# Two attentions in one fused kernel: heads issued in pairs, values as the stationary operand, constant rows moved into the second MLP

## The chip, the cores and the metric

The kernel runs on one core of one Trainium2 chip. The metric is the device time of one execution in microseconds (us). The core has a matrix engine (TensorE, PE in the profile, with its weight loads on a row of their own, PEld), a vector engine (VectorE, DVE), a scalar engine (ScalarE, ACT), GpSimd (POOL) and SyncE (SP), which issues all DMAs here. Each has its own queue, in order, and they meet by semaphores. [...]

## The reference

Three models of one layer each follow one another on 1024 positions of 1024 channels, all in fp32: a gated linear attention block with an MLP, a block with two attentions, a convolution and a gated MLP, and a block of spatial gating and pooling with an MLP. The change is in the second. Its attentions are these:

```python
def forgetting_attention(q, k, v, log_f):          # "fox": 6 heads of 64, blocks of 128 queries
    c = cumsum(log_f)                              # per head, over positions
    s = q @ k.T / 8 + c[query] - c[key]; s = where(key <= query, s, -inf)
    return softmax(s) @ v

def dilated_branch(q, k, v, window, dilation):     # (128, 1), (512, 4), (2048, 16)
    # blocks of window // dilation positions taken at steps of dilation, each with the one before
    s = where(band & ~first, q @ k.T / 8, -inf)
    m = max(s); e = exp(s - m); l = sum(e)
    return e @ v, m, l

def dilated_mixture(q, k, v):                      # 6 heads of 64
    a_p = exp(m_p - max_p(m_p))                    # weight of each of the three branches
    return sum_p(a_p * num_p) / sum_p(a_p * l_p)
```

Both outputs (384 channels each) go through an RMS norm with gains, are joined with 256 channels of the convolution and multiplied by w_o. Then comes an MLP of 2 x 2816 channels up and 2816 down. The third model's projections have a bias made of sums over rows of weights times the vector `mod`; there are 44 blocks of such weights, the constant rows.

## The kernel before, in words

Activations stand with channels on partitions and 1024 positions along the free side. A large product is a `job`: for each of 8 blocks of 128 channels three products of split parts (whi by hi, whi by lo, wlo by hi; L449, L450, L455) into one of three PSUM slots of two banks, `ps[0..2]`, taken in turn by `take`. A further slot of two banks, `misc`, holds small things. Weights come through a ring of four buffers `raw`; ACT rounds them into `whi` and POOL makes `wlo`.

The dilated attention (L719 to L778 on PE) has 72 units, `DUN`: a branch, a block of queries, a pair of heads. Unit n has its scores (two heads in the halves of the rows, L728), the mask added by a matmul of an identity with `negm` (L731), the maximum on DVE (L1832), the exponential with its sum on ACT from PSUM (L1242), transposes on PE (L716), a copy to SBUF on ACT or DVE (L1228, L1446), and the product with the values (L746). In the last, the transposed weights are stationary (128 columns) and 64 channels of values stream, so the output has positions on partitions. PE issues the scores of unit n, the transposes of n - 2 and the values of n - 3 in one step. Every three units a block of 128 positions by 384 channels, with maxima and sums, goes to DRAM through the three tiles `T` (24 stores). Six gate groups (`cn`, L754) and 44 row sums lie between the units: POOL multiplies a block of weights by `mod` and folds it with three additions (L2160), and PE sums over partitions with a column of ones (L774).

Fox (L781 to L829) has 48 units, `FUN`: a block of queries i (from 7 down to 0) and one head, against i + 1 blocks of keys. It has scores (L791), the causal mask (L792), gates and maximum in one DVE instruction (L1866), exponential on ACT (L1267), i + 1 transposes, copies and values (L803). Beside it run the eight `join` steps that read the dilated blocks back from DRAM, mix the three branches (POOL, L2160), and turn them on PE (L810), as are fox's own outputs. Norm factors are spread over channels by `spread` (L476): DVE first makes a diagonal block product of 1024 columns (`diag`, L1468), and PE multiplies it by ones. This helper is used for the norms of all three models.

The order of every queue is written out by hand, by the same loops over the same lists on each engine; the only freedom is what a wait leaves. The first model's MLP takes 48 blocks `ada` along, of the same kind as the constant rows, at the places `ADA_AT`: POOL multiplies, DVE sums over k (L1701), PE sums over partitions with ones (L630).

## Time and profile before

| | us |
|---|---|
| median of 3 runs (lowest, highest) | 3929.88 (3917.98, 3930.02) |
| the profiled execution's own time | 3927.38 |
| its span | 3925.5 |
| PE busy | 3749.1 (96%) |
| DVE / ACT / POOL busy | 1551.9 (40%) / 1006.5 (26%) / 1373.6 (35%) |
| mean granted clock of PE | 0.933 |

The page cuts the span into 40 slices of 98 us and gives each one digit, in tenths. PE stands at 9 in nearly all. The line of the granted clock (`PEclk`) reads 9 in most, and 8, 6, 5, 9 and 5 in the five slices between 1570 and 2061 us; the attentions lie between 1614 and 2045 us. A busy PE at a clock of 0.5 does half of the work in a microsecond. The chain that ended last is 89% PE.

One fp32 matmul of the source is two instructions in the trace, each a weight load and a stream that takes two passes over its columns. Durations of PE instructions overlap; what one costs is the distance from start to start.

### The profile page before, as it was taken

The numbers are of one execution on the slowest core, as the hardware profiler recorded it, in microseconds if no ns is written. First come the engines' busy times: TensorE is split into PE (matmuls) and PEld (weight loads), VectorE is DVE, ScalarE is ACT, GpSimd is POOL, SyncE is SP. The second block draws the span as 40 slices with busy tenths as digits, with TensorE's granted clock in tenths as the row PEclk, the third lists the DMA queues.
The fourth block names the chain that finished last, engine by engine and source line by source line (L and its number), as shares of the span: only waits on it lengthen the run. The fifth ranks groups of instructions, "written<-read, shape, count | busy, mean of one in ns | idle before, by whom it ended". The sixth has DMA issues, their size and how long they took to land.

```text
span 3925.5 us, 39427 instructions
## 1 busy us (share of the span) xinstructions
PE 3749.1 (96%) x16958; PEld 3039.1 (77%) x16958; DVE 1551.9 (40%) x1446; ACT 1006.5 (26%) x1460; POOL 1373.6 (35%) x786
## 2 busy tenths in 40 slices
PE   7999899999999999999989999999999979999997
PEld 5787678888888777777768778888877758888885
DVE  4444334333333466222434443433345351222224
ACT  4221122111111311343432322222242332222211
POOL 2111124444444422487322323332244343333332
PEclk9898889999999999865959999999999979999998
DMA  2011222222222211244102111111111111111112
GB/s 93 27 54 38 81 75 68 89 83 90 81 85 83 86 62 43 90 128 135 38 15 77 41 51 49 39 51 57 38 63 38 43 65 49 47 46 47 49 49 108
DMA packets 86107, 250.29 MB, mean 64 GB/s; under 512 B 9367, under 2 KB 18343, under 8 KB 85677
## 3 DMA queue, kind: packets, MB, share of 16 engines
q1 hardware_dynamic: 85932, 247.77, 19.1%
q8 instruction: 134, 2.20, 0.2%
q14 instruction: 41, 0.33, 0.0%
HBM read 224.52 MB, written 23.22 MB: 63 GB/s over the span
## 4 chain that ended last, share of the span: by engine, by line
PE 89%; DVE 6%; ACT 2%; POOL 2%; issue 1%; DMA 0%; SPq 0%; DVEq 0%; ACTq 0%
PE ps L449 25%; PE ps L455 25%; PE ps L450 25%; PE ps L791 2%; PE ps L716 2%; PE ps L803 1%; PE ps L746 1%; PE ps L728 1%; PE ps L542 1%; POOL raw L2160 1%; DVE T L1440 1%; PE ps L476 1%; DVE HL L1456 1%; DVE T L1465 1%; PE ps L607 1%
## 5 line engine op out<-in xcount | busy, mean ns | idle before, releaser
L2154 POOL TENSOR_TENSOR wlo<-raw,whi 128x1024 fp32r<-128x1024 f32 (+3 forms) x368 | 697.3, 1895 | 1836.1 <-ACT whi L926 1675.5
L449 PE MATMUL ps<-HH,whi 128*128 128x512 f32 (+2 forms) x2816 | 1125.7, 400 | 69.5 <-DVE HL L1456 30.7
L450 PE MATMUL ps<-HL,whi 128*128 128x512 f32 (+2 forms) x2816 | 1113.2, 395 | 0.0
L455 PE MATMUL ps<-HH,wlo 128*128 128x512 f32 (+2 forms) x2816 | 891.6, 398 | 0.0
L926 ACT ACTIVATE whi<-raw 128x1024 fp32r<-128x1024 f32 (+3 forms) x368 | 311.5, 847 | 1896.5 <-PE ps L455 1866.3
L449 PEld LDWEIGHTS ps<-HH,whi 128*128 128x128 f32 (+2 forms) x2816 | 536.2, 190 | 202.1 <-DVE HL L1456 29.5
L449 PE MATMUL ps<-GH,whi 128*128 128x512 f32 x1600 | 628.6, 393 | 7.9 <-POOL wlo L2154 7.8
L450 PEld LDWEIGHTS ps<-HL,whi 128*128 128x128 f32 (+2 forms) x2816 | 536.0, 190 | 116.6 <-issue 3.0
L450 PE MATMUL ps<-GL,whi 128*128 128x512 f32 x1600 | 623.6, 390 | 0.0
L455 PEld LDWEIGHTS ps<-HH,wlo 128*128 128x128 f32 (+2 forms) x2816 | 525.0, 190 | 105.1
L455 PE MATMUL ps<-GH,wlo 128*128 128x512 f32 x1600 | 494.1, 390 | 0.0
L1440 DVE TENSOR_TENSOR X<-ps,X 128x1024 f32<-128x1024 f32 x184 | 224.9, 1223 | 563.6 <-PE ps L455 560.0
L449 PEld LDWEIGHTS ps<-GH,whi 128*128 128x128 f32 x1600 | 301.7, 189 | 72.4 <-issue 10.5
L455 PEld LDWEIGHTS ps<-GH,wlo 128*128 128x128 f32 x1600 | 301.1, 188 | 62.9
L450 PEld LDWEIGHTS ps<-GL,whi 128*128 128x128 f32 x1600 | 301.2, 188 | 62.3 <-issue 0.8
L2160 POOL TENSOR_TENSOR GL<-T,GH 128x1024 fp32r<-128x1024 f32 x86 | 206.8, 2406 | 354.8 <-ACT GH L1127 236.8
L1451 DVE TENSOR_TENSOR T<-ps,RT 128x1024 f32<-128x1024 f32 x72 | 88.0, 1223 | 353.5 <-PE ps L455 319.4
L1701 DVE TENSOR_REDUCE adat<-raw 128x128 f32<-128x1024 f32 x48 | 97.0, 2022 | 236.1 <-POOL raw L2160 236.1
L1443 DVE SCALAR_TENSOR_TENSOR T<-T,cols,T 128x1023 f32<-128x1023 f32 x88 | 136.8, 1554 | 59.5 <-ACT T L1323 58.0
L1440 DVE TENSOR_TENSOR T<-ps,RT 128x1024 f32<-128x1024 f32 (+2 forms) x34 | 41.6, 1224 | 289.3 <-PE ps L455 260.5
L1127 ACT ACTIVATE GH<-T 128x1024 fp32r<-128x1024 f32 x64 | 68.0, 1062 | 269.1 <-DVE T L1440 269.1
L1440 DVE TENSOR_TENSOR T<-T 128x1024 f32<-128x1024 f32 (+3 forms) x74 | 112.7, 1523 | 40.2 <-ACT T L1119 39.1
(323 smaller groups left out, 3428.9 us busy)
## 6 DMA issues: line engine op xcount, KB each, us to landing
raw<-in_w_up SPq DMA_DIRECT2D x76, 512.0 KB, 3.3
raw<-in_w_in SPq DMA_DIRECT2D x70, 512.0 KB, 3.3
raw<-in_w_fc SPq DMA_DIRECT2D x64, 512.0 KB, 3.4
raw<-in_w_down SPq DMA_DIRECT2D x104, 256.0 KB, 2.7
raw<-in_w_ada SPq DMA_DIRECT2D x48, 512.0 KB, 3.5
raw<-in_w_fc SPq DMA_DIRECT2D x64, 256.0 KB, 2.7
X<-in_xT SPq DMA_DIRECT2D x16, 512.0 KB, 7.2
raw<-in_w_out SPq DMA_DIRECT2D x16, 512.0 KB, 3.3
```

Source lines behind the costliest of these rows:

```text
L449: e.matmul(o_[0:m, half(hf)], whi_[:, k, :], hi[k0 + k][:, half(hf)], start=first, stop=False)
L450: e.matmul(o_[0:m, half(hf)], whi_[:, k, :], lo[k0 + k][:, half(hf)], start=False, stop=False)
L455: i = e.matmul(o_[0:m, half(hf)], wlo_[:, k, :], hi[k0 + k][:, half(hf)], start=False, stop=last)
L716: i = e.transpose(o_[:, blk(j)], src[:, blk(j)], ident[:])
L791: e.matmul(o_[:, 512 * hf:512 * hf + k], QA[r_, t_, blk(i_)], KA[r_, t_, 512 * hf:512 * hf + k], start=True, stop=hf != (P * i_) // 512)
L926: e.activation(whi_of(name), raw_of(name), ACT.Copy).then_inc(*ac.inc("hi " + name))
L1440: e.tensor_tensor(o, a, b, op).then_inc(*dv.inc(*names))
L1443: e.scalar_tensor_tensor(out=o, in0=a, scalar=s_, in1=b, op0=op0, op1=op1).then_inc(*dv.inc(*names))
L1451: e.tensor_tensor(dst, ps[slot[g]][:], RT[:], MUL).then_inc(*dv.inc("free " + g, *names))
L1701: e.tensor_reduce(adat[:, f % 2, :], raw_of(f"ada{f}").rearrange("p (k m) -> p m k", k=8), AX.X, ADD).then_inc(*dv.inc(f"red ada{f}"))
L2154: e.tensor_tensor(wlo_of(name), raw_of(name), whi_of(name).bitcast(F), SUB).then_inc(*po.inc("lo " + name))
L2160: e.tensor_tensor(o, a, b, op).then_inc(*po.inc(*names))
```

## The change

- Dilated units run with eight blocks of one branch and head pair after the other. The mask matmul goes: DVE reads scores from PSUM and the mask from SBUF in one instruction per head, which writes the negated masked scores to SBUF and their minimum to `ML`. ACT takes the exponential from SBUF, in place. Scores alternate between `ps[0]` and `ps[1]`, transposes use the halves of `ps[2]`.
- Values are stationary (64 columns), the transposed weights stream (128 columns), the two heads go to the two halves of the output partitions. Outputs have channels on partitions and are copied into `NUM` at their positions; only maxima and sums go through DRAM (`msc`), 36 numbers per position.
- Fox runs by pairs of heads and halves of the queries, `FUN`, in 36 steps over the key blocks, `FSTEP`. Scores of both heads alternate; the exponentials of four query blocks lie in SBUF (`PF`); a step turns one key block for up to four query blocks and both heads, ACT copies the one head and DVE the other, and values are stationary with up to 512 columns streaming. The first four score pairs go behind the last dilated units.
- Mixing weights, softmax sums and norm factors are spread over channels by matmuls that take a broadcast column as stationary and the identity as moving operand, one such group in most steps (`FSIDE`); DVE multiplies them in. `spread` takes the same form for all norms of the kernel, and `diag` goes everywhere.
- The constant rows go into the second MLP at `ROW_AT`, in the way of `ada`; their loads stand there in the order of the weights.

```diff
+ROW_AT = [n for n in range(3, 62) if n % 4]
...
-DUN = [(br, u, t_) for br in range(3) for u in range(8) for t_ in range(3)]
-FUN = [(i, hd) for i in range(7, -1, -1) for hd in range(6)]
+DUN = [(br, t_, u) for br in range(3) for t_ in range(3) for u in range(8)]
+DSEQ = []
+for _n in range(len(DUN)):
+    DSEQ.append(("unit", _n))
+    if _n % 12 == 5:
+        DSEQ.append(("gate", _n // 12))
+FUN = [(t_, qd) for t_ in range(3) for qd in (1, 0)]
+FSTEP = [(k, j) for k in range(6) for j in range(8 if FUN[k][1] else 4)]
+FSCORE = {}
+for _k in range(5):
+    for _x, _i in enumerate(range(4 * FUN[_k + 1][1] + 3, 4 * FUN[_k + 1][1] - 1, -1)):
+        FSCORE[FSTEP.index((_k, 2 * _x + 1 if FUN[_k][1] else _x))] = (_k + 1, _i)
+FSIDE = {}
+_spread = [("mix", t_, br, hf) for t_ in range(3) for br in range(3) for hf in range(2)]
+for _n, (_k, _j) in enumerate(FSTEP):
+    if _k and _j == 0:
+        FSIDE[_n] = [("out", _k - 1)]
+    elif _n > 1 and _spread:
+        FSIDE[_n] = [_spread.pop(0)]
+_late = [n for n in range(len(FSTEP)) if n > max(n for n in FSIDE if FSIDE[n][0][0] == "mix") + 2 and n not in FSIDE]
+FSIDE[_late[2]] = [("rd sum",)]
+FSIDE[_late[3]] = [("rd", 0)]
+FSIDE[_late[4]] = [("rd", 1)]
+FSIDE[33], FSIDE[34] = [("rf sum", 1)], [("rf", 1)]
+SIDES = [x for n in sorted(FSIDE) for x in FSIDE[n]] + [("out", 5), ("rf sum", 0), ("rf", 0)]
...
+        def by_act(n):
+            br, t_, u = DUN[n]
+            return has_prev(br, u) == 1 and u % 3 == 0
...
+        def before_scores(k, i_):
+            if (k, i_) == (0, 7):
+                return dv("dm71")
+            lo = 4 * FUN[k][1]
+            if i_ < lo + 3:
+                return dv(f"fm{k} {i_ + 1}")
+            return dv(f"fm{k - 1} {4 * FUN[k - 1][1]}")
...
+            def spread(g, r, tok):
+                o_ = take(g)
+                q.wait_ge(*tok)
+                for b in range(8):
+                    i = e.matmul(o_[:, blk(b)], r[:, b:b + 1].broadcast_to([P, P]), ident[:], start=True, stop=True)
                 i.then_inc(*pe.inc(g))
...
             def dscores(n):
-                br, u, t_ = DUN[n]
+                br, t_, u = DUN[n]
                 pv_ = has_prev(br, u)
                 w = P * (1 + pv_)
-                o_ = take(f"ds{n}", f"ds{n - 1}")
+                side_by(("unit", n))
                 if n == 0:
                     q.wait_ge(*dv("kb2"))
                 for hh in range(2):
                     r_ = slice(64 * hh, 64 * hh + 64)
-                    e.matmul(o_[:, 512 * hh:512 * hh + w], dtok(QB[r_, t_, :], br, u, 0), dtok(KB[r_, t_, :], br, u, pv_), start=True, stop=False)
-                mk = 2 if br == 2 else 1 - pv_
-                for hh in range(2):
-                    i = e.matmul(o_[:, 512 * hh:512 * hh + w], identb[:], negm[:, mk:mk + 1 + pv_, :].rearrange("p a b -> p (a b)"), start=False, stop=True)
+                    i = e.matmul(dslot(n)[:, 512 * hh:512 * hh + w], dtok(QB[r_, t_, :], br, u, 0), dtok(KB[r_, t_, :], br, u, pv_), start=True, stop=True)
                 i.then_inc(*pe.inc(f"ds{n}"))
...
+            def side_by(x):
+                i = DSEQ.index(x)
+                if i > 1:
+                    what, m = DSEQ[i - 2]
+                    q.wait_ge(*(dv(f"dm{m}") if what == "unit" else ac(f"cn{m}")))
+                elif held[i]:
+                    q.wait_ge(*freed(held[i]))
...
+            def dturn(n):
+                br, t_, u = DUN[n]
+                q.wait_ge(*ac(f"dp{n}"))
+                if n > 1:
+                    q.wait_ge(*at_of(f"dq{n - 2}"))
+                elif held[2]:
+                    q.wait_ge(*freed(held[2]))
+                at_ = 512 * (n % 2)
+                for j in range(2 * (1 + has_prev(br, u))):
+                    i = e.transpose(ps[2][:, at_ + P * j:at_ + P * j + P], pd[n % 3][:, blk(j)], ident[:])
+                i.then_inc(*pe.inc(f"dT{n}"))
+            def dpv(n):
+                br, t_, u = DUN[n]
+                nb, g = 1 + has_prev(br, u), n // 8
+                q.wait_ge(*at_of(f"dq{n}"))
+                if u % 4 == 0:
+                    if g:
+                        q.wait_ge(*at_of(f"nu{g - 1} {u // 4}"))
+                    else:
+                        q.wait_ge(*dv("yc mean1"))
+                        q.wait_ge(*ac("nl sd"))
+                    if t_ == 0:
+                        q.wait_ge(*(ac("vbT2"), dma["v4"]("v4 1"), dma["v16"]("v16"))[br])
+                for j in range(nb):
+                    v_ = (VB[:, (u - nb + 1 + j) % 8, :], V4[:, (4 * (u // 4 - nb + 1 + j) + u % 4) % 8, :], V16[:, u, :])[br]
+                    for hh in range(2):
+                        hd = 2 * t_ + hh
+                        i = e.matmul(misc[64 * hh:64 * hh + 64, blk(u)], v_[:, 64 * hd:64 * hd + 64], qd_[n % 3][:, blk(nb * hh + j)], start=(j == 0), stop=(j == nb - 1))
+                i.then_inc(*pe.inc(f"dpv{n}"))
+            def scores(k, i_):
+                t_, qd = FUN[k]
+                w = P * (i_ + 1)
+                q.wait_ge(*before_scores(k, i_))
+                if k == 0:
+                    q.wait_ge(*dv("ka2"))
+                    q.wait_ge(*ac("cn5"))
+                for hf in range(-(-w // 512)):
+                    n = min(512, w - 512 * hf)
+                    for hh in range(2):
+                        r_ = slice(64 * hh, 64 * hh + 64)
+                        e.matmul(ps[hh][:, 512 * hf:512 * hf + n], QA[r_, t_, blk(i_)], KA[r_, t_, 512 * hf:512 * hf + n], start=True, stop=hf != i_ // 4)
+                for hh in range(2):
+                    i = e.matmul(ps[hh][:, blk(i_)], identb[:], negm[:, 1, :], start=False, stop=True)
+                i.then_inc(*pe.inc(f"fs{k} {i_}"))
...
+            for s_i in range(n + 4):
                 if s_i < n:
                     dscores(s_i)
+                    if s_i % 12 == 5:
+                        gate_sums(s_i // 12)
...
+            def fturn(n):
+                k, j = FSTEP[n]
+                qd = FUN[k][1]
+                q.wait_ge(*ac(f"fp{k} {4 * qd}"))
+                for hh in range(2):
+                    if n:
+                        q.wait_ge(*(dv if hh else ac)(f"fq{n - 1}"))
+                    else:
+                        q.wait_ge(*at_of("dq70"))
+                        q.wait_ge(*at_of("dq71"))
+                    for i_ in range(max(j, 4 * qd), 4 * qd + 4):
+                        at_ = 512 * hh + P * (i_ - 4 * qd)
+                        i = e.transpose(ps[2][:, at_:at_ + P], PF[i_, hh][:, blk(j)], ident[:])
+                    i.then_inc(*pe.inc(f"fT{n} {hh}"))
+            def fpv(n):
+                k, j = FSTEP[n]
+                t_, qd = FUN[k]
+                c0 = P * max(0, j - 4 * qd)
                 if n == 0:
-                    q.wait_ge(*dv("ka2"))
-                for hf in range(-(-w // 512)):
-                    k = min(512, w - 512 * hf)
-                    e.matmul(o_[:, 512 * hf:512 * hf + k], QA[r_, t_, blk(i_)], KA[r_, t_, 512 * hf:512 * hf + k], start=True, stop=hf != (P * i_) // 512)
-                e.matmul(o_[:, blk(i_)], identb[:], negm[:, 1, :], start=False, stop=True).then_inc(*pe.inc(f"fs{n}"))
-
-            def fox_pv(n):
-                i_, hd = FUN[n]
-                at_ = 512 * (i_ % 2) + 64 * hd
-                q.wait_ge(*at_of(f"fq{n}"))
-                if n == 0:
+                    q.wait_ge(*at_of("nu8 0"))
                     q.wait_ge(*ac("vaT2"))
-                if hd == 0:
-                    q.wait_ge(*(dv(f"f{i_ + 2}") if i_ < 6 else dv(f"do{22 + i_ - 6}")))
-                for j in range(i_ + 1):
-                    i = e.matmul(misc[:, at_:at_ + 64], q2[n % 2][:, blk(j)], VA[:, j, 64 * hd:64 * hd + 64], start=(j == 0), stop=(j == i_))
+                elif j == 0:
+                    q.wait_ge(*ac(f"fo{k - 1}"))
+                q.wait_ge(*ac(f"fq{n}"))
+                q.wait_ge(*dv(f"fq{n}"))
+                for hh in range(2):
+                    hd = 2 * t_ + hh
+                    i = e.matmul(misc[64 * hh:64 * hh + 64, c0:512], VA[:, j, 64 * hd:64 * hd + 64], T[n % 3][:, 512 * hh + c0:512 * hh + 512], start=(j == 0), stop=(j == 4 * qd + 3))
                 i.then_inc(*pe.inc(f"fpv{n}"))
...
+                if x[0] == "mix":
+                    t_, br, hf = x[1:]
+                    q.wait_ge(*dv("mix w"))
+                    for b in range(4):
+                        for hh in range(2):
+                            c_ = 2 * t_ + hh
+                            i = e.matmul(misc[64 * hh:64 * hh + 64, 512 + P * b:640 + P * b], WD[:, 4 * hf + b, br, c_:c_ + 1].broadcast_to([P, 64]), ident[:], start=True, stop=True)
...
+            n = len(FSTEP)
+            for s_i in range(n):
+                if s_i in FSCORE:
+                    scores(*FSCORE[s_i])
+                fturn(s_i)
+                if s_i:
+                    fpv(s_i - 1)
+                for x in FSIDE.get(s_i, ()):
+                    side(x)
+            fpv(n - 1)
+            side(("out", 5))
...
+            def row2_step(n):
+                for f in rows:
+                    if f == 0:
+                        q.wait_ge(*ac("fo5"))
+                    q.wait_ge(*dv(f"red b{f}"))
+                    e.matmul(misc[:, f:f + 1], adat[:, f % 2, :], ones[:, 0:1], start=True, stop=True).then_inc(*pe.inc(f"brow{f}"))
+                rows.clear()
+                if n in ROW_AT:
+                    rows.append(ROW_AT.index(n))
...
+            def dmax(n):
+                br, t_, u = DUN[n]
+                pv_ = has_prev(br, u)
+                w = P * (1 + pv_)
+                q.wait_ge(*pe(f"ds{n}"))
+                q.wait_ge(*(pe(f"dT{n - 3}") if n > 2 else pe("ka2")))
+                for hh in range(2):
+                    c_ = 2 * t_ + hh
+                    e.tensor_tensor_reduce(out=pd[n % 3][:, w * hh:w * hh + w], in0=dslot(n)[:, 512 * hh:512 * hh + w], in1=dmask(br, pv_), scale=-1.0, scalar=3.0e38, op0=ADD, op1=MIN, accum_out=ML[:, br, u, c_:c_ + 1]).then_inc(*dv.inc(f"dm{n}" if hh else f"dm{n}a"))
...
+                for hh in range(2):
+                    e.tensor_tensor_reduce(out=PF[i_, hh], in0=ps[hh][:, 0:w], in1=CN[:, 2 * t_ + hh, 0:w], scale=-1.0, scalar=3.0e38, op0=ADD, op1=MIN, accum_out=FM[:, k % 2, i_ % 4, hh:hh + 1]).then_inc(*dv.inc(f"fm{k} {i_}" if hh else f"fm{k} {i_}a"))
...
+            def row2_step(n, name):
+                if n in ROW_AT:
+                    f = ROW_AT.index(n)
+                    row_tile(f"b{f}", mod[:, 0:8] if f < 12 else mod[:, 24:32], dv("mod"))
+                    lows(widx[name] + 3)
...
+            for br in range(3):
+                q.wait_ge(*ac(f"dp{24 * br + 23}"))
+                if br == 0:
+                    load("ml", msc[:, 0:12].rearrange("(u p) c -> p u c", p=P), ML[:, 0], "ml0")
+                    q.wait_ge(*pe("dpv23"))
+                    load("v16", V16[:], vsc.rearrange("(j u) c -> j u c", u=8), "v16")
+                elif br == 1:
+                    for n in range(2):
+                        load("ml", msc[512 * n:512 * n + 512, 12:24].rearrange("(p r) c -> p r c", r=4), ML[:, 1, 4 * n:4 * n + 4, :], f"ml1{n}")
+                else:
+                    load("ml", msc[:, 24:36].rearrange("(p u) c -> p u c", u=8), ML[:, 2], "ml2")
+            q.wait_ge(*dma["ml"]("ml2"))
+            load("mn", MN[:], msc.rearrange("(i p) (b c) -> p i b c", p=P, b=3), "mn")
```

## Rows read from the trace of the kernel before

**Rows 1.** The page, part 1: busy us and share of each engine.
```profile
PE 3749.1 (96%) x16958; PEld 3039.1 (77%) x16958; DVE 1551.9 (40%) x1446; ACT 1006.5 (26%) x1460; POOL 1373.6 (35%) x786
```
**Rows 2.** Windows: stretch, length, busy PE, PEld, DVE, ACT, POOL; clock, DMA share, GB/s.
```profile
1614.30:1841.60 227.30, 217.79 (x1175) 174.09 (x1174) 67.59 (x164) 93.53 (x344) 177.31 (x165) 0.66 0.43 138
1841.60:2045.30 203.70, 190.34 (x897) 133.18 (x897) 86.61 (x210) 80.12 (x178) 49.93 (x52) 0.73 0.09 27
620.00:1000.00 380.00, 377.63 (x1689) 312.40 (x1688) 143.33 (x99) 59.95 (x70) 185.39 (x98) 1.00 0.26 85
```
**Rows 3.** Windows, PE alone: stretch, length, busy, clock, DMA share, GB/s.
```profile
1700.00:1735.00 35.00, 34.40 (x156) 0.50 0.40 126
1865.00:1945.00 80.00, 79.13 (x522) 1.00 0.13 39
1955.00:2000.00 45.00, 45.00 (x156) 0.50 0.00 1
```
**Rows 4.** Timeline of PE, two dilated units: start us, us, line, instructions.
```profile
1614.30 0.49 PE L728 MATMUL ps<-KB,QB 64*128 64x128 f32 x4
1614.72 0.28 PE L731 MATMUL ps<-negm,identb 128*128 128x128 bf16 x2
...
1648.67 0.70 PE L728 MATMUL ps<-KB,QB 64*128 64x256 f32 x4
1649.31 0.39 PE L731 MATMUL ps<-negm,identb 128*128 128x256 bf16 x2
1649.54 0.60 PE L716 MATMUL ps<-ident,p 128*128 128x128 f32 x4
1649.97 1.00 PE L746 MATMUL ps<-VB,q 128*128 128x64 f32 x8
1650.91 0.49 PE L728 MATMUL ps<-KB,QB 64*128 64x256 f32 x2
```
**Rows 5.** Timeline of PE in the first model: key and value products.
```profile
425.49 0.71 PE L455 MATMUL ps<-HH,wlo 128*128 128x512 f32 x2
426.13 1.09 PE L564 MATMUL ps<-V,KDT 128*64 128x128 f32 x16
```
**Rows 6.** Timeline of PE in the first MLP, ahead of a row sum.
```profile
1271.07 0.62 PE L455 MATMUL ps<-GH,wlo 128*128 128x512 f32 x2
1271.53 0.28 PE L630 MATMUL ps<-ones,adat 128*128 128x1 f32 x2
```
**Rows 7.** Timeline of all engines, its PE rows: a fox unit.
```profile
1863.13 1.98 PE L791 MATMUL ps<-KA,QA 64*128 64x512 f32 x4
...
1865.11 1.05 PE L716 MATMUL ps<-ident,p 128*128 128x128 f32 x8
...
1865.99 1.90 PE L803 MATMUL ps<-VA,q 128*128 128x64 f32 x16
```
**Rows 8.** Groups by line and form: count, busy us, mean ns, idle before and releasers.
```profile
L1866 DVE CUSTOM_DVE_ANT_0 s<-ps,CN 128x1024 f32<-128x1024 f32 x6 | 7.3, 1216 | 12.5 <-PE ps L792 12.5
L1866 DVE CUSTOM_DVE_ANT_0 s<-ps,CN 128x256 f32<-128x256 f32 x6 | 2.4, 418 | 1.1 <-PE ps L792 1.1
...
L1242 ACT ACTIVATE p<-ps,T 128x256 f32<-128x256 f32 x66 | 30.8, 474 | 36.7 <-DVE T L1832 34.0 <-issue 2.6
L1242 ACT ACTIVATION_READ_ACCUMULATOR p<-ps,T 128x1 f32 x144 | 29.2, 203 | 0.0
```
**Rows 9.** DMA issues up to 1842 us: count, KB each, median us to landing.
```profile
cm<-dsc SPq DMA_DIRECT2D x1, 594.0 KB, 4.2
```
**Rows 10.** Waits of PE: waiting line, releaser, us in total, times, longest.
```profile
PE ps L476 <- DVE T L1468: 12.7, 4, 7.1
```
**Rows 11.** Timeline of PE: the transposes that waited, ahead of the fall of the clock.
```profile
1948.74 0.77 PE L716 MATMUL ps<-ident,p 128*128 128x128 f32 x5 [0.93 <-DVE st L1866]
```
**Rows 12.** Timeline of PE in the first model: two shapes in turn at 1.2 GHz.
```profile
478.89 0.79 PE L606 MATMUL ps<-V,AT 128*128 128x128 f32 x2
479.61 0.79 PE L607 MATMUL ps<-SA,QI 64*128 64x128 f32 x2
```

754 lines of the change are left out of this document (367 added, 387 removed).

## The prediction

> **What bounds the kernel now.** Read first the busy shares of the page: TensorE (PE) is busy for 3749.1 of 3925.5 us [rows 1], so a change pays only where it shortens PE's queue or its waits. The windows by stage come next, since PE's clock is not the same in all: the dilated attention takes 227.3 us at a mean granted clock of 0.66, the forgetting ("fox") attention with the wait behind it, up to the first matmul of w_o, 203.7 us at 0.73; a stretch of the first MLP, for comparison, has 1.00 [rows 2]. The two attentions take 431.0 us together. No other engine is near full: POOL, the nearest, has 177.3 us of 227.3 [rows 2]. Narrower windows show two states in them: 45 us (1955 to 2000) and 35 us (1700 to 1735) at 0.50, with PE counted busy throughout, and 80 us (1865 to 1945) at 1.00 [rows 3]. 0.50 is 1.2 GHz, 1.00 is 2.4 GHz. So I price PE's work at 2.4 GHz and then ask what clock it gets.
>
> **PE's work in the dilated attention.** There are 72 units (a block of queries, two heads), 33 with a previous block and 39 without. At 2.4 GHz the starts of a unit with one give scores 0.64, mask 0.23, transposes 0.43, values 0.94 us, 2.24 in all [rows 4]. A unit without costs 0.42 for scores (its first two rows) and half of the rest, about 1.25. The sum of these, 74 + 49, with 88 row matmuls of some 0.12 and six gate groups of 1.9 (1024 columns in four instructions, as fox's scores in rows 7), gives 145; 227.3 x 0.66 gives 150, so the model holds.
> - Removed: the masks (they become an operand of VectorE) and the 44 row sums.
> - Kept: scores 33 x 0.64 + 39 x 0.42 = 37.5, 210 transposes x 0.107 = 22.5, gate groups 11.5.
> - Values: before, each instruction loads 128 columns of weights to stream 64; 8 take 0.94 us, 0.118 each. After, 64 columns are loaded and 128 streamed, the heads alternating between the halves of the output partitions. The first model already has this shape: 16 such instructions start within 1.09 us, 0.055 each beyond the first [rows 5], half of 128 x 2 / 2.4 GHz = 0.107. So (n + 1)/2 x 0.107: 0.48 for a unit with a previous block, 0.27 without; 33 x 0.48 + 39 x 0.27 = 26.4 in place of some 51.
> - Entering that shape: the two matmuls ahead of it take 0.64 to the next start where 0.46 is usual [rows 5, 6], 0.18 more; another entry showed less, so 0.13 x 72 = 9.
> The sum is 107 us at 2.4 GHz, 43 less than the 150.
>
> The Trainium skill, TensorEngine Tiling, section Key Properties, says that changing the tiling mode drains TensorE. The scores (64 rows) to mask (128 rows) step shows no such drain: 0.64 is 3 x 0.213, three streams of 256 columns in two passes, with nothing over [rows 4]. By the rule each of three mode changes per unit would cost something; a rival below works that out from two shapes of this trace.
>
> **PE's work in fox.** At 2.4 GHz, 1024 columns of scores for one head take 1.98 with their mask, 8 transposes 0.88, 16 value instructions 1.9 [rows 7]; that is 46 + 5 + 23 + 51 over all heads, some 10 more for turning the rows back.
> - Scores in pairs: the halves of the rows alternate as in the dilated unit, whose four instructions took three slots. A pair then takes, for 1024 columns, 3 x 0.427 + 2 x 0.427 = 2.13 instead of 3.8; over the eight widths 10.45 us, three times 31.4. Masks stay at 5, transposes at 23.1.
> - Values: 36 steps of two heads, up to 512 columns streamed per instruction, four instructions in three slots: 34.6. The entries at 0.13 add 5.
> - New: 18 groups of 16 instructions that spread the mixing weights, 8.5 x 0.107 = 0.91 each, 16.4; six for the softmax sums, 5.5; sums of squares, 64 weight-bound instructions at 0.118, 7.5; four groups that spread factors, 3.5.
> The sum is 133 us (I use 132), about what there was (203.7 x 0.73 = 149 with the waits in it). So fox gains from its clock and its end, and hardly from its work.
>
> **The other engines.** After, DVE does two reduces of 256 columns (0.42 each) and a copy of 512, by the same rows some 0.68: 1.5 to 1.7 for a unit with a previous block; ACT two exponentials with read-out, 2 x 0.68 = 1.35, and ACT takes nine of the copies [rows 8]. PE's 1.68 is level with this, so units go at 1.8. Without a previous block 1.2 of ACT and DVE stands against 1.03 + 0.13 of PE: 1.25. These are floors at 2.4 GHz; at 1.2 GHz PE needs 3.3 and 1.95 and hides them. Scores leave PSUM by DVE alone, so a slot is free sooner.
> - Seam: the first four score pairs of fox all use the same two slots and each waits for DVE's two reduces of the one before. PE 8.0, DVE 2 x 1.22 for the widest [rows 8], 8.8 for four, one after the other: PE idles some 12 us. The maxima and sums go through DRAM with one store and one load behind the last dilated unit; the load of before took 4.2 us [rows 9], two such legs lie inside the 17 us of the seam. If they took 10 each, DVE would hold its copies and PE some 5 us.
> - In fox DVE's copies and PE's next transposes share one slot; the value step (1.28) covers a 512-column copy. I take 8 for late ones, of 0 to 25.
> - End: PE waited for up to 7.1 us at the last factors [rows 10] in a tail of about 12. After, the dilated parts are split first, but w_o still waits for copy, high part and low part, and later for the last factors: 11.
>
> **The clock.** Before, units with a previous block and fox's wide rows ran mostly at 2.4 GHz, those without, and everything behind PE's 0.93 us wait at 1948, at 1.2 for tens of us [rows 3, 11]. The value instructions of before stream in 0.053 of 0.118 us; the new ones stream without a gap, on both halves, and fox streams 512 columns. I expect fox at a mean of 0.9, 132/0.9 = 147, dilated units with a previous block at 2.1, those without half and half at 1.65: 69 + 64 + 15 for the gates = 148. With 12 + 8 + 11 the stages take 326, 105 less. The bounds of this term are the rivals.
>
> **What is moved.** 44 row groups go into the second MLP: a load of 512 KB on SP's queue, one POOL multiplication, one DVE reduce, two small matmuls. The first MLP carries 48 of the same; PE is busy there 377.6 of 380 us [rows 2]. On PE one is two instructions bound by their weight load, 0.118 each as the values of before [rows 4]: 44 x 0.24 = 10. DVE and POOL have the room; but DVE reduces stand ahead of PSUM readers, and the loads ahead of weights in the ring of four buffers: 4 more, 32 at the worst. Nothing removed hides it: +14. The diagonal products that the spreads waited for go: 12.7 us of waits in all [rows 10], 7.1 of them in the end above; I take 4 of the other 5.6, of 0 to 5.6. The three rotating tiles are not staging the outputs any more, which takes 24 stores and 8 loads off SP; they hid behind PE and I count nothing.
>
> **Sum.** -105 + 14 - 4 = -95. The profiled execution took 3927.4 us (span 3925.5), so 3832; the median of the runs is 3929.9, 2.5 above it: 3835.
>
> **Rivals.**
> - *Full clock* (0.20). The denser streams hold 2.4 GHz: dilated 33 x 1.8 + 39 x 1.25 + 12 = 120, fox 132 + 12 + 8 + 10: 282, 149 less; 3790. For it: 1865 to 1945, where PE never waits. Against: the dilated units leave PE short gaps.
> - *Clock as before* (0.15). 107/0.66 + 8 = 170 and 132/0.73 = 181, 33 around them: 384, 47 less; 3893.
> - *Drains at mode changes* (0.06). Two shapes that alternate in the first model start 0.72 us apart for two instructions at 1.2 GHz, against 0.43 of streaming [rows 12]: 0.29 a change, 0.15 at full clock. Three changes in each of 108 steps at 0.2 are 65, 14 of which are in the sum: 3886. Against: the scores above.
> - *The clock stays down* (0.09), the side of slower. PE, done sooner, waits for DVE and ACT in most units, and falls to 1.2 GHz as after 1948, and the units keep it there as from 1955 to 2000. Then 33 x 3.3 + 39 x 1.95 + 23 = 208, fox 264 + 35: 507, 76 more; with the 10 outside 4016. It decides from a mean clock of 0.61 downwards: 239/0.61 + 31 = 421. For it: the wait at 1948 and what came behind it [rows 3, 11]. Against: in the 80 us at 2.4 GHz up to 1945 the stream was scores, transposes and values too.
> The skill, TensorE: Matmul & The Clock Gate, Part 4, says that a transpose doesn't count as activity for the clock. Their share of PE's work rises, from 15 to 21% in the dilated units; by that rule the last two clock rivals gain. No row here separates it.
>
> **Chances.** The forecast has 0.50, its own range is 3800 to 3870. The range 3780 to 3905 takes in all rivals but the last. A measurement of this kernel tells 0.3% from no change, 12 us: faster 0.88, same 0.03, slower 0.09.
>
> **What would show it.** Value instructions (128*64) some 0.055 us apart at 2.4 GHz; PE's clock above 0.85 between the stages; a seam with some 12 us of PE waits for DVE's reduce; 40 to 50 us less in the dilated windows even at the same clock; the second MLP 10 to 15 us longer. The forecast is wrong if fox is at 0.5 for long, if the mode changes show gaps, or if PE in the second MLP waits for a row's buffers.

## The result and the profile after

The changed kernel takes 3862.2 us (median of 4 runs, 3860.1 to 3869.9), the kernel before 3928.6 on the same chip: a ratio of 0.984, 95% interval 0.9818 to 0.9863. The forecast was 3835, faster, in a range of 3780 to 3905. The profiled execution has a span of 3861.5, against 3925.5: 64.0 less.

The page of the kernel after, its part 1 (busy time, share of the span, instructions; it answers to [rows 1]):

```profile
PE 3659.0 (95%) x17082; PEld 2938.8 (76%) x17082; DVE 1628.3 (42%) x1657; ACT 992.2 (26%) x1407; POOL 1244.2 (32%) x614
```

Windows of the kernel after: the dilated attention up to fox's first scores, fox up to the first matmul of w_o, and the second MLP up to the first matmul of the pooling (stretch, its length, then busy time of PE, PEld, DVE, ACT, POOL with instruction counts; granted clock, DMA share, GB/s). The first two answer to [rows 2].

```profile
1611.70:1778.90 167.20, 159.51 (x933) 90.29 (x932) 83.99 (x360) 87.47 (x313) 2.35 (x1) 0.75 0.07 24
1778.90:1924.70 145.80, 128.22 (x1012) 77.82 (x1010) 79.75 (x189) 71.83 (x153) 21.24 (x9) 0.91 0.01 2
2035.30:2897.20 861.90, 819.03 (x3610) 675.17 (x3609) 399.97 (x296) 221.43 (x227) 330.48 (x170) 0.97 0.23 72
```

The second MLP of the kernel before, between the same two instructions, which the rows ahead of the prediction do not have:

```profile
2146.40:2957.50 811.10, 794.45 (x3497) 654.21 (x3496) 324.22 (x253) 223.29 (x227) 249.19 (x126) 0.99 0.15 48
```

These give the whole account, worked out from the borders of the windows:

| part | before | after | difference | forecast |
|---|---|---|---|---|
| up to the first dilated score | 1614.3 | 1611.7 | -2.6 | 0 |
| dilated attention | 227.3 | 167.2 | -60.1 | 148 |
| fox, seam and end | 203.7 | 145.8 | -57.9 | 147 + 12 + 8 + 11 = 178 |
| w_o, up to the second MLP | 101.1 | 110.6 | +9.5 | 0 |
| second MLP | 811.1 | 861.9 | +50.8 | +14 |
| the rest | 968.0 | 964.3 | -3.7 | -4 |
| span | 3925.5 | 3861.5 | -64.0 | -95 |

The attentions gave more than forecast (-118 against -105), but by two errors that cancel in part: the dilated one gave 19 less, fox 32 more. The second MLP cost more (+51 against +14).

A unit with a previous block of the first branch after, at a clock of 1.00 (timeline of PE: start, duration as modelled, line, instructions). It answers to [rows 4]; a price is the distance from start to start.

```profile
1629.60 0.70 PE L812 MATMUL ps<-KB,QB 64*128 64x256 f32 x4
1630.23 0.66 PE L842 MATMUL ps<-ident,T 128*128 128x128 f32 x4
1630.82 0.66 PE L862 MATMUL ps<-T,VB 128*64 128x128 f32 x8
1631.41 0.70 PE L812 MATMUL ps<-KB,QB 64*128 64x256 f32 x4
```

Scores 0.63, transposes 0.59, values 0.59: 1.81, where the forecast had 1.8. The values went from 0.94 to 0.59. The transposes, the same four 128x128 blocks, went from 0.43 to 0.59.

Units of the second and third branch cost more, and neither [rows 4] nor the lines above show that. Here is a unit without a previous block of the third branch, at 1.00 (run 3 below) and at 0.50 (the kernel after):

```profile
1743.23 0.84 PE L813 MATMUL ps<-KB,QB 64*128 64x128 f32 x4
1744.00 0.44 PE L843 MATMUL ps<-ident,T 128*128 128x128 f32 x2
1744.37 0.44 PE L863 MATMUL ps<-T,V 128*64 128x128 f32 x4
```

```profile
1747.64 0.85 PE L812 MATMUL ps<-KB,QB 64*128 64x128 f32 x4
1748.42 0.69 PE L842 MATMUL ps<-ident,T 128*128 128x128 f32 x2
1749.03 0.70 PE L862 MATMUL ps<-T,V 128*64 128x128 f32 x4
1749.66 0.85 PE L812 MATMUL ps<-KB,QB 64*128 64x128 f32 x4
```

Its transposes and values take 0.37 each at 1.00 and 0.61 and 0.63 at 0.50, but its scores take 0.77 and 0.78: the same at both clocks, where the same four instructions take 0.42 in the first branch at 1.00. A unit of the second branch with a previous block (run 12 below, at 1.00) has scores of 1.21 for 0.63:

```profile
1704.28 1.28 PE L813 MATMUL ps<-KB,QB 64*128 64x256 f32 x4
1705.49 0.66 PE L843 MATMUL ps<-ident,T 128*128 128x128 f32 x4
```

The kernel before has it too: 1.21 at 1727 us, where the clock is 0.50, and 1.21 at 1743, where it is 1.00. In the source these scores differ from those of the first branch in one thing: they take queries and keys at steps of 4 or 8 positions, the first branch neighbouring ones. No run changes the steps alone.

The waits of PE in the second MLP after (who waited, for what; us in total, times, longest). Before, the only like one was the wait for `wlo`, 8.8 us in 6.

```profile
PE ps L997 <- DVE adat L1886: 18.6, 7, 5.7
PE ps L540 <- POOL wlo L2353: 16.3, 7, 3.1
```

### The profile page after: what moved, and what is told of

It is laid out like the page before. It is cut to its first block, busy times and chain, and to the rows that moved or that the text cites. A ratio compares the mean times of both kernels' runs of the same rounds, so it can differ in the third digit from the quotient of the medians.

```text
span 3861.5 us, 39442 instructions
## 1 busy us (share of the span) xinstructions
PE 3659.0 (95%) x17082; PEld 2938.8 (76%) x17082; DVE 1628.3 (42%) x1657; ACT 992.2 (26%) x1407; POOL 1244.2 (32%) x614
## 4 chain that ended last, share of the span: by engine, by line
PE 90%; DVE 6%; ACT 2%; POOL 1%; issue 1%; DMA 0%; SPq 0%; DVEq 0%; ACTq 0%
PE ps L540 26%; PE ps L546 26%; PE ps L541 26%; PE ps L812 1%; PE ps L842 1%; PE ps L862 1%; PE ps L632 1%; PE ps L877 1%; DVE T L1634 1%; DVE T L1659 1%; DVE HL L1650 1%; PE ps L566 1%; PE ps L697 1%; PE ps L924 1%; PE ps L908 1%; PE ps L696 1%
## 5 line engine op out<-in xcount | busy, mean ns | idle before, releaser
L540 PE MATMUL ps<-GH,whi 128*128 128x512 f32 x1536 | 610.7, 398 | 16.4 <-POOL wlo L2353 13.1
L541 PE MATMUL ps<-GL,whi 128*128 128x512 f32 x1536 | 602.4, 392 | 0.0
L546 PE MATMUL ps<-GH,wlo 128*128 128x512 f32 x1536 | 478.8, 393 | 0.0
L540 PEld LDWEIGHTS ps<-GH,whi 128*128 128x128 f32 x1536 | 292.7, 191 | 76.7 <-POOL wlo L2353 14.2
L546 PEld LDWEIGHTS ps<-GH,wlo 128*128 128x128 f32 x1536 | 292.3, 190 | 61.8
L541 PEld LDWEIGHTS ps<-GL,whi 128*128 128x128 f32 x1536 | 291.5, 190 | 58.7
L1886 DVE TENSOR_REDUCE adat<-raw 128x128 f32<-128x1024 f32 x92 | 185.5, 2016 | 263.3 <-POOL raw L2359 263.2
```

Source lines behind the costliest of these rows:

```text
L540: e.matmul(o_[0:m, half(hf)], whi_[:, k, :], hi[k0 + k][:, half(hf)], start=first, stop=False)
L541: e.matmul(o_[0:m, half(hf)], whi_[:, k, :], lo[k0 + k][:, half(hf)], start=False, stop=False)
L546: i = e.matmul(o_[0:m, half(hf)], wlo_[:, k, :], hi[k0 + k][:, half(hf)], start=False, stop=last)
L1886: e.tensor_reduce(adat[:, f % 2, :], raw_of(name).rearrange("p (k m) -> p m k", k=8), AX.X, ADD).then_inc(*dv.inc("red " + name))
```

## The experiments

Twelve runs. Where no span is given, times are medians. Ratios are against the kernel before on the same chip; differences are against 3862.2. These cross chips: the kernel before took 3928.6 beside the changed kernel, 3927.4 to 3927.7 beside runs 1 to 8, but 3923.1 beside runs 9, 10 and 12 and 3920.6 beside run 11, so a difference of these four carries some 5 to 8 us of the chip. The lengths of stages below come from the traces.

**1. The rows left out.** The 44 constant rows are not computed, the bias is zero.

```diff
-ROW_AT = [n for n in range(3, 62) if n % 4]
+ROW_AT = []
```

> The kernel after, with the 44 constant rows left out altogether (loads, multiplications, sums and matmuls; the third block's bias is zero). The stretch from the second MLP's first norm sums to the first pool matmul was 811.1 us before and is 861.9 after. Theory A (the rows hold buffers of the weight ring behind the convolutions on DVE, so PE waits for rows and weights and loses its clock): it comes back to 811 to 814, the kernel to about 3812 (-50). Theory B (only the rows' own PE work is due to them, 44 x 0.24 = 10 us, the rest is something else, as the attention's end or another order of the buffers): -10 to -15, 3849.

Measured 3817.7, ratio 0.9718 [0.9699, 0.9737], 44.5 less, nearest theory A. The waits for `adat` are gone, and those for `wlo` are the 8.8 us in 6 of before. Between the first matmul of w_o and the pooling it takes 924.3 us; the kernel after takes 972.5, the kernel before 912.2. So 48 of the 60 us that this stretch became longer are the rows, and 12 are not. Nearly all of the 48 are in the second MLP, which takes 813.7 at 0.99 here (811.1 before); w_o takes the 110.6 of after.

**2. The rows moved within the MLP.** The same 44, none at the last up step of a group of the MLP or at the first down step.

```diff
-ROW_AT = [n for n in range(3, 62) if n % 4]
+ROW_AT = sorted([3, 4] + [12 * g + x for g in range(1, 5) for x in (2, 3, 4)] + [12 * g + 6 + x for g in range(5) for x in (1, 2, 3, 5, 6, 7)])
```

> The kernel after, with the same 44 rows at other places of the same MLP: none at the last up step of a group nor at the first down step behind it, three at the other up steps, six of eight down steps. All work is the same. Theory A (each of the five waits of 3.0 + 2.4 us stands at such a last up step, where DVE's row sum queues behind the convolution and holds a buffer): these waits go, and with them the time at 1.2 GHz behind them: -20 to -30 us, 3835 to 3842. Theory C (the ring of four buffers is too short for any such density of rows): the waits only move, within 8 us of 3862.

Measured 3837.1, ratio 0.977 [0.9753, 0.9787], 25 less, with all the rows still computed. Waits of PE in that MLP:

```profile
PE ps L540 <- POOL wlo L2353: 14.4, 10, 5.2
PE ps L997 <- DVE adat L1886: 1.9, 3, 0.8
```

So more than half of the rows' price was where they stood. What is left, 19.4 against the run without them, is 10.4 of PE's own (88 instructions at 0.118), 5.6 more of waits for `wlo` and 1.9 for `adat`, and some 1.5 unassigned.

**3. The gate groups moved forward**, behind units 5, 9, 13, 17, 21 and 29 in place of 5, 17, 29, 41, 53 and 65.

```diff
-    if _n % 12 == 5:
-        DSEQ.append(("gate", _n // 12))
+    if _n in GATE_AT:
+        DSEQ.append(("gate", GATE_AT.index(_n)))
```

> The kernel after, with the six gate groups (6 rows of 128 streaming) behind dilated units 5, 9, 13, 17, 21, 29 in place of 5, 17, 29, 41, 53, 65. All work is the same. Theory A (the clock falls behind each gate group, and units without a previous block can't bring it back, so the two groups in the third branch cost far more than their 2 us): the third branch, 1733 to 1779 in the profile, runs mostly at 2.4 GHz in place of 1.2, 24 units x 0.7: -12 to -17 us, about 3848. Theory B (units without a previous block are at 1.2 GHz whatever stands between them): within 5 us of 3862, the third branch at 0.5.

Measured 3849.7, ratio 0.9798 [0.9782, 0.9813], 12.5 less. Windows over the third branch, the kernel after first, then this run:

```profile
1735.00:1778.90 43.90, 41.86 (x194) 22.46 (x194) 20.31 (x95) 18.77 (x76) 0.00 (x0) 0.50 0.00 1
```

```profile
1735.00:1763.00 28.00, 28.00 (x187) 17.60 (x188) 18.28 (x98) 17.50 (x75) 0.00 (x0) 1.00 0.00 1
```

Both windows hold 18 to 19 of the branch's 24 units. They take 28 us at 1.00 in place of 44 at 0.50. Not all of the 16 is the clock: the window after also holds a gate group (3.7) and the wait for its read-out (2.0), which this run has earlier; the units themselves go from 2.02 to 1.51 each. The dilated attention as a whole went from 167.2 at 0.75 to 151.4 at 0.91.

**4. The dilated values in the old form**, all else as after: transposed weights stationary, 64 columns of values moving. Later steps work on other numbers here and in runs 6, 10 and 11.

```diff
-e.matmul(misc[64*hh:64*hh+64, blk(u)], v_[:, 64*hd:64*hd+64], qd_[n % 3][:, blk(nb*hh+j)], ...)
+e.matmul(misc[:, P*u+64*hh:P*u+64*hh+64], qd_[n % 3][:, blk(nb*hh+j)], v_[:, 64*hd:64*hd+64], ...)
```

> The kernel after, with the value products of the dilated units as they were before the change: transposed weights stationary (128 columns), values moving (64 columns), output with positions on partitions (so the later steps work on other numbers). Everything else is as after. Theory A (start distances of 0.118 in place of 0.055 us, 420 instructions): 26 us more PE work at 2.4 GHz, less the entries and exits of the 64-column shape (72 x 0.26 = 19), so only 5 to 10 us more at full clock, more if the clock falls with it: +10 to +25. Theory B (the value products gain their full 26 to 40 us, mode changes cost nothing): +26 to +45.

Measured 3914.3, ratio 0.9973 [0.9959, 0.9987]: 52 more, above both expectations. The dilated attention takes 215.8 (from 1615.3 to 1831.1), 48.6 more, at a clock of 0.57. A unit of it at full clock:

```profile
1655.30 0.70 PE L812 MATMUL ps<-KB,QB 64*128 64x256 f32 x4
1655.93 0.66 PE L842 MATMUL ps<-ident,T 128*128 128x128 f32 x4
1656.42 1.00 PE L862 MATMUL ps<-VB,T 128*128 128x64 f32 x8
1657.36 0.49 PE L812 MATMUL ps<-KB,QB 64*128 64x128 f32 x4
```

It takes 2.06, only 0.25 more than the new form: values 0.94 against 0.59, but transposes 0.49 against 0.59. A unit without a previous block at 1.2 GHz takes 2.14 against 2.02. So the work that the new form saves is 33 x 0.25 + 39 x 0.12 = 13 us. The other 35 are put down to the clock. It fell at about 1626, behind the first gate group (1623), came back at about 1650, and fell again at about 1667, just behind a wait of 1.6 for a gate group's read-out; from 1690 to 1815 it was 0.50 in every window.

**5. Rows moved and gates forward together.**

> The changed kernel with both edits: the 44 row groups at the second MLP's steps except the last up step and the first down step of a group, and the six gate groups behind units 5, 9, 13, 17, 21 and 29 of the dilated attention. Theory A, the two losses are apart (buffers held by rows in the second MLP; the clock behind the gates in the attention): the gains add, -25 and -12.5 to -19, so 3819 to 3826, with the mean clock between the start of the dilated attention and the first matmul of w_o above 0.9. Rival B: a higher clock in the attention shows again as a lower one later, or the two overlap: 3832 to 3840, no better than the rows alone.

Measured 3823.2, ratio 0.9738 [0.9716, 0.976], 39 less: the two gains (25 and 12.5) add.

**6. Old form of the dilated values, gates forward.**

> The dilated values in the form of the kernel before (transposed weights stationary, 64 columns of values moving; later steps then work on other numbers), and the six gate groups moved forward as in the run of the early gates (3849.7). With the gates in their old places this form cost 52 more than the changed kernel, at a mean clock of 0.57 in the dilated attention. Theory A, the form itself takes the clock away (it streams 64 of the columns of each load only): the third branch, which has no gates now, stays near 0.5, and the time is 40 to 55 above 3850, 3890 to 3905. Rival B, the gates bring the clock down and the form costs only its work (about 24 at full clock): third branch above 0.9, 3873 to 3880.

Measured 3924.6, ratio 1.0 [0.9987, 1.0012], 75 more than run 3: beyond both expectations, on the side of A. Two windows of it, the second from behind the last gate group (1726 to 1730) to the end of the stage:

```profile
1640.00:1665.00 25.00, 23.40 (x80) 15.44 (x80) 5.53 (x22) 7.19 (x24) 0.00 (x0) 0.50 0.00 1
1730.00:1840.00 110.00, 110.00 (x496) 91.33 (x494) 48.52 (x212) 44.07 (x174) 0.00 (x0) 0.50 0.01 1
```

The clock falls at about 1626, as in run 4, but here the next groups start at 1639, 1658, 1677, 1696 and 1726, and it does not come back: it is 0.50 in every window up to 1840, over 210 us; the last 110 of these are without a gate group and with PE busy throughout. Moving the gates forward makes the old form worse, the new one better. With the gates in the same places the new form (run 3) comes back each time, mostly after 3 to 4 us, and holds 1.00 through the third branch.

**7. The spreads of the mixing weights cut to a quarter**, 17 of the 18 groups (part of the mixing is left out).

> The changed kernel, 17 of the 18 groups that spread the mixing weights of the dilated branches (16 matmul instructions, about 1.0 each) cut to a quarter; part of the mixing weights is left out. Theory A: TensorE bounds this stage, so the 204 instructions go from the end, at 0.06 each: -11 to -13, 3849 to 3851. Rival B: they fill TensorE's waits for the softmax steps and the copies of the fox attention, and little or nothing goes: 3857 to 3863. Below A: without them the clock falls or rises; a move of more than 16 would show that.

Measured 3856.3, ratio 0.9823 [0.9795, 0.985]: 6 less, between the two. Fox takes 137.0 from its first scores to w_o in place of 145.8, so 8.8 of the 12 came off, and PE's waits there for VectorE's `FM` rose from 6.0 to 8.7. That about a quarter of the spreads' work was under a wait is a reading of these two numbers; the kernel's 6 us would make it half.

**8. Fox's scores one head after the other.**

```diff
-                for hf in range(-(-w // 512)):
-                    n = min(512, w - 512 * hf)
-                    for hh in range(2):
-                        r_ = slice(64 * hh, 64 * hh + 64)
+                for hh in range(2):
+                    r_ = slice(64 * hh, 64 * hh + 64)
+                    for hf in range(-(-w // 512)):
+                        n = min(512, w - 512 * hf)
```

> The changed kernel, the scores of a pair of heads in the fox attention issued one head after the other (all columns of head one, then of head two) in place of alternating between the halves of the rows. Theory A: two matmuls on different halves of the rows overlap, and the order decides it: 144 instruction pairs lose one slot in four or more; 10.45 for one pair of heads over the eight widths becomes about 15, times three +13, 3874 to 3877. Rival B: the overlap comes from the form (64 rows each) and not from the order, or the waits for VectorE hide it: 3860 to 3865.

Measured 3863.5, ratio 0.9848 [0.9821, 0.9875]: no difference, rival B. The widest pair of the kernel after, then of this run:

```profile
1824.46 1.99 PE L877 MATMUL ps<-KA,QA 64*128 64x512 f32 x8
1826.38 0.28 PE L879 MATMUL ps<-negm,identb 128*128 128x128 bf16 x2
```

```profile
1824.00 1.99 PE L877 MATMUL ps<-KA,QA 64*128 64x512 f32 x8
1825.93 0.28 PE L879 MATMUL ps<-negm,identb 128*128 128x128 bf16 x2
```

Eight instructions of 0.427 take 1.92 in either order, 4.5 slots. In order and one ahead, the second order could overlap only one, and would take 7 slots, 2.99. So each half of the rows works through its own instructions. My term took that overlap for a matter of order, with three slots for four instructions. Fox's eight widths show what it is. Three of them, each with the mask behind it as the next start:

```profile
1816.48 0.70 PE L877 MATMUL ps<-KA,QA 64*128 64x256 f32 x4
1817.12 0.28 PE L879 MATMUL ps<-negm,identb 128*128 128x128 bf16 x2
```

```profile
1822.14 0.49 PE L877 MATMUL ps<-KA,QA 64*128 64x128 f32 x4
1822.56 0.29 PE L879 MATMUL ps<-negm,identb 128*128 128x128 bf16 x2
```

```profile
1833.70 1.56 PE L877 MATMUL ps<-KA,QA 64*128 64x512 f32 x8
1835.19 0.29 PE L879 MATMUL ps<-negm,identb 128*128 128x128 bf16 x2
```

For 128, 256, 768 and 1024 columns of each head the distances are 0.42, 0.64, 1.49 and 1.92. Streaming on both halves at once takes 0.21, 0.43, 1.28 and 1.71 of them (an instruction of 128 columns takes 0.107, and there are two for each head). What is over is 0.21 each time, whatever the width. So a group of scores costs n/2 slots and a fixed 0.21 at its end; whether that is a drain at the change from 64 to 128 rows or the end of the last pair, these rows do not tell.

**9. The gate groups over 128 rows**, in their places of after; 122 rows are zero.

```diff
-        SEL = at("SEL", RO, [6, 6, P])
+        SEL = at("SEL", RO, [P, 6, P])
...
-SEL[0:6, hd, :], CF[0:6, half(hf)]
+SEL[:, hd, :], CF[:, half(hf)]
...
+            e.memset(CF[:], 0.0).then_inc(*dv.inc("cf0"))
...
+            e.memset(SEL[:], 0.0).then_inc(*dv.inc("sel0"))
```

> The changed kernel; the six gate groups of the dilated attention, in their old places, contract over 128 rows (122 of them zero) in place of 6. The same 1024 columns in four instructions, so the same 1.92 of TensorE at full clock; VectorE has two more memsets of about 1 ahead of the attention. Theory A, the six-row groups are what lets the granted clock fall: behind them it stays at 1.00, the clock of the dilated attention rises from 0.75 to 0.9 or more and 10 to 20 go: 3843 to 3853. Rival B, it falls for the waits for their read-out (1.6 and 2.0 on ScalarE) or for other reasons: 0.75 stays, 3860 to 3866.

Measured 3847.0, ratio 0.9803 [0.9788, 0.9818], 15 less (some 10 with the chips set right): theory A. Two stretches, the kernel after first:

```profile
1670.00:1700.00 30.00, 30.00 (x177) 16.86 (x174) 16.05 (x66) 15.91 (x57) 0.00 (x0) 0.89 0.11 44
1730.00:1760.00 30.00, 30.00 (x136) 16.08 (x135) 14.18 (x71) 14.11 (x59) 0.00 (x0) 0.53 0.01 1
```

```profile
1670.00:1700.00 30.00, 30.00 (x180) 17.16 (x181) 16.23 (x70) 17.40 (x64) 0.00 (x0) 1.00 0.12 49
1730.00:1760.00 30.00, 27.96 (x170) 16.86 (x168) 15.83 (x83) 17.28 (x68) 0.00 (x0) 0.88 0.00 1
```

The dilated attention takes 149.4 (from 1615.6 to 1765.0) at 0.90. The same waits for the read-out are there (5.8 us in 4), and its clock still falls three times, at about 1654, 1705 and 1753, for 3, 14 and 14 us: each time within 2 us of the end of a wait of 1.6 or 2.0 us for a read-out (1652.5, 1705.1, 1753.7). In the kernel after it fell within or right behind the groups at 1644, 1672, 1700 and 1731, before the wait for the read-out of each. So the waits bring the clock down as well, and rival B had part of it.

**10. Fox's values in the old form.**

> The changed kernel, only the values of the fox attention in the form of before (the transposed weights stationary in blocks of 128 columns, 64 columns of values moving; later steps work on other numbers). Work at full clock: 216 matmuls of two instructions of 0.118 make 51, against 0.91, 0.69, 0.48 and 0.27 for the four widths after, 25 in all: +26. Theory A, as in the dilated attention the form takes the clock as well (0.91 in the stage now, 0.73 before): the stage takes 145.8 + 26 at about 0.7, 190 to 225, time 3905 to 3940. Rival B, with fox's wide scores beside it the clock holds at about 0.9: +26 to +32, 3888 to 3894.

Measured 3885.5, ratio 0.99 [0.9883, 0.9918]: 23 more (some 29 with the chips set right), at rival B. Fox takes 161.6 at 0.93, 16 more than after. Here the form costs work, and the clock is not lower.

**11. Old form of the dilated values, gates over 128 rows.**

> The changed kernel with the dilated values in the form of before (3914 with the gates as they are) and the gate groups over 128 rows in their old places (3847 with the new form of the values); later steps work on other numbers. In both runs with the old form the clock went to 0.50 behind a gate group of six rows and stayed there to the end of the dilated attention. Theory A, this form lets the clock fall by itself: mean below 0.65 again, 3900 to 3915. Rival B, the form only keeps it from coming back, and it is the six-row groups that bring it down: with them gone the clock is above 0.85 and what is left is the form's work, some 0.25 in each unit with a previous block and 0.15 in the others: 3855 to 3870.

Measured 3880.0, ratio 0.9887 [0.9852, 0.9922]: between the two. The dilated attention takes 177.1 at 0.78; against run 9 the form costs 33 (13 of work by the rows above), against run 4 the wide gates give 34. So both matter. The clock falls three times here, at about 1655, 1723 and 1778, each within 2 us of the end of a wait of 1.6 to 2.0 for a read-out, as in run 9; but it stays down for 34, 31 and 17 us, where run 9 had 3, 14 and 14. The old form does not bring the clock down here, it keeps it down. Twice it came back at a gate group of 128 rows; this is the first time:

```profile
1683.34 0.69 PE L842 MATMUL ps<-ident,T 128*128 128x128 f32 x2
1683.82 0.95 PE L862 MATMUL ps<-V,T 128*128 128x64 f32 x4
```

```profile
1685.91 3.56 PE L830 MATMUL ps<-CF,SEL 128*128 128x512 f32 x4
1689.30 0.38 PE L842 MATMUL ps<-ident,T 128*128 128x128 f32 x2
1689.52 0.56 PE L862 MATMUL ps<-V,T 128*128 128x64 f32 x4
```

Two transposes take 0.48 ahead of it and 0.22 behind it. The group itself took 3.39 to the next start; at full clock it takes 1.82.

**12. Rows moved, gates forward and over 128 rows.**

> Rows moved off the two steps and gate groups moved forward (3823.2), and the gates over 128 rows as well. Theory A (six rows let the clock fall): the clock of the dilated attention rises from 0.87 to 0.9 to 0.97 or more, 4 to 12 go: 3811 to 3819. Rival B: no difference, 3820 to 3826.

Measured 3815.6 (3812.3 to 3822.2), ratio 0.9728 [0.9707, 0.9749]: the fastest version, 47 faster than the changed kernel (some 41 with the chips set right). The dilated attention takes 142.8 at 0.98, against 154.3 in run 5. The gain of the kernel over run 5 is 7.6, in theory A's range, but the chips differ by 4.6 the same way, so it is shown by the stage and not by the median.

## Why the prediction was right, and where not

The outcome and the range held, and the time lies in the forecast's own 3800 to 3870, near its upper end. The terms in it did so less well: against the forecast the dilated attention is 19 too long, fox 32 too short, w_o 9.5 and the second MLP 37 too long. That the sum is only 31 off is luck in part. Of the signs that I had named for being wrong, one came true, PE waiting in the second MLP for a row's buffers; and the clock, which I had above 0.85, was 0.75 in the dilated attention and 0.91 in fox.

- **What bounds it.** Right: PE's work and its clock. Which of the two is the larger was not. Of the forecast's 79 us in the dilated attention 43 were work at full clock. Of the 60 measured 48.6 go back when its values alone return to the old form, and of these 13 are work and some 35 clock (run 4).
- **Dilated units of the first branch.** The unit at full clock was right (1.8, measured 1.81), partly by luck: the floor that I gave to DVE and ACT is PE's own time. The steps between shapes were under-priced, 0.13 for the way in alone: the same four transposes take 0.43 with the mask ahead of them [rows 4], 0.49 right behind the scores (run 4) and 0.59 with the new values behind them, so 0.06 and 0.10; the values take 0.59 for 0.43 of streaming (8 x 0.107 / 2), 0.16 over, part of which may be the way out. The scores have 0.21 over (run 8), where I read "three streams ... with nothing over": 0.64 is two streams of 0.213 and this step. So the row that I held against the rival of drains does not speak against it. In all, 0.53 of the unit's 1.81 is over the streaming, near the three times 0.2 of that rival; but the 0.21 was in the kernel before as well, so as a price of the change 0.6 was too high. The Trainium skill, TensorEngine Tiling, Key Properties, says that a change of tiling mode drains TensorE. The 0.10 ahead of the new values agrees with it, at half of the 0.2 that the rival had for each of three, and so may the 0.21 behind the scores.
- **Dilated units of the second and third branch.** This is the step that failed in the dilated attention: 148 forecast, 167.2 measured. I priced all scores by rows of the first branch, 0.64 and 0.42, 37.5 in all. In the other branches they take 1.21 and 0.77, at either clock: 21 x 0.63 + 3 x 0.42 + 12 x 1.21 + 36 x 0.77 = 57, 19 more. A unit without a previous block was forecast at 1.25 and takes 1.51 at full clock; its scores alone take 0.35 more than I had; DVE and ACT are busy for 0.65 and 0.63 of that window (run 3), so neither is full. "So the model holds", 145 against 227.3 x 0.66 = 150, was luck: the same scores were as long in the kernel before, and time that does not follow the clock can't be multiplied by it.
- **The dilated clock** cost about what was forecast. The stage takes 142.8 at 0.98 (run 12), 24 less than after at 0.75; my 148 stood 28 above the 120 of the rival at full clock. But the cause was not named. I had counted the gate groups as 11.5 us of work and not asked what they do to the clock. Runs 3 and 9 show that they bring it down: moved or widened, 16 to 18 us of the stage go. What is left of the falls in run 9 stands behind waits for their read-out.
- **Fox** was forecast too long: 178 with its seam and end, measured 145.8. Three sizes were off. The values take 0.91 for four instructions of 512 columns, not 1.28: two slots and 0.06, so both column halves run wholly beside each other, and 36 steps make 25, not 34.6. The scores of 1024 columns take 1.92, not 2.13, by the same reason (run 8), some 28 in all, not 31.4. Both were three slots for four where two and a fixed step are right. And the waits are 17 us (6.0 for DVE's minima, 5.8 for the exponentials, about 2 for copies, 3.2 for w_o's operand), not 31. The seam was right in kind and too large: I had 12 us of waits for DVE's reduces, and there are three of 5.3 together and one for ACT of 2.7, in 21 us:

```profile
1785.52 2.35 PE L877 MATMUL ps<-KA,QA 64*128 64x512 f32 x8 [1.76 <-DVE FM L2045]
1790.40 2.93 PE L877 MATMUL ps<-KA,QA 64*128 64x512 f32 x8 [1.58 <-DVE FM L2045]
1795.54 1.35 PE L877 MATMUL ps<-KA,QA 64*128 64x512 f32 x8 [1.94 <-DVE FM L2045]
1799.90 0.47 PE L908 MATMUL ps<-ident,P 128*128 128x128 f32 x1 [2.69 <-ACT P L1421]
```

- **"44 row groups ... 4 more, 32 at the worst".** This is the term that was mis-sized: +50.8 for the second MLP against +14, beyond even the bound with PE's 10. Run 1 gives the rows 44.5. The mechanism was named (DVE's reduces ahead of readers of PSUM, the memory for PE's results, and loads ahead of weights in the ring), but priced by the first MLP, where nothing like the convolution stands on DVE. Timeline of DVE, of PE, and of ACT at the end of one group of the kernel after (idle time before an instruction, and what ended it, in brackets):

```profile
2298.25 2.60 DVE L1637 SCALAR_TENSOR_TENSOR T<-T,cols,T 128x1023 f32<-128x1023 f32 x2 [1.31 <-ACT T L1515]
2300.88 1.23 DVE L1634 TENSOR_TENSOR T<-T,T 128x1024 f32<-128x1024 f32 x1
2302.03 1.93 DVE L1886 TENSOR_REDUCE adat<-raw 128x128 f32<-128x1024 f32 x1
```

```profile
2304.01 0.38 PE L997 MATMUL ps<-ones,adat 128*128 128x1 f32 x2 [2.97 <-DVE adat L1886]
2306.90 0.80 PE L540 MATMUL ps<-GH,whi 128*128 128x512 f32 x1 [2.50 <-POOL wlo L2353]
```

```profile
2308.02 0.63 ACT L1090 ACTIVATE whi<-raw 128x512 fp32r<-128x512 f32 x1 [4.30 <-DMA raw<-in_w_down]
```

  The reduce queues on DVE behind the convolution. PE's own queue waits for it (2.97). The reduce also holds one of the four weight buffers, so the next `w_down` is loaded late, ACT waits for it, and PE again (2.50). With rows at these steps PE waits 18.6 + 16.3 - 8.8 = 26 us more; with PE's 10.4 that is 36.5 of 50.8. The other 14 fit the clock, 0.97 in place of 0.99 over 862 us, which is 17 at most; without the rows it is 0.99 again (run 1). Run 2 takes the rows off these steps and gets 25 back.
- **w_o, +9.5, had no term.** At its start stand fox's last sums and factors, which before were ahead of it; it stays at 110.6 without the rows (run 1). By the timeline these are 24 sums (2.6), a spread (0.8), waits of 1.9 and 0.6 for the joined operand and a lower clock; no run takes them apart.
- **The diagonal products**, -4: measured -3.7 in all that is neither the attentions, w_o nor the second MLP. Not tested by itself.

## What to carry to other kernels

A short group of matmuls with few contraction rows can cost more in the clock of the next tens of us than in its own time; where the clock is low behind one, try it over all rows (zeros will do) or move it into denser work before touching the units themselves. A matmul form is worth its work plus what it does to the clock, and the second can be the larger: test it in place. Price a unit from a row of its own branch: matmuls of one shape differed by nearly two here where they read at steps, and that part did not follow the clock. When small work is moved into a stage, look in that stage for the step where the in-order engine that it uses is already the last one, and leave that step out.
